# VectorE's block sums of a w_ada load: four instructions in a row, or two halves with a weight remainder between them

## The chip, the cores and the metric

The kernel runs on one core of one Trainium2 chip. The metric is the time of one execution on the device in microseconds (us), of which the median over several executions is compared. The core has a matrix engine (TensorE, PE in the profile), VectorE (DVE), ScalarE (ACT), GpSimd (POOL) and SyncE (SP), each with its own stream of instructions, which meet by semaphores. Transfers from HBM are started by an engine (here by SyncE and by ScalarE) and run on the core's DMA engines.

## The reference

Two transformer blocks in float32 on 256 tokens of width 2048. The first block (eight attention heads of 128 and a gated convolution of 1024 channels) is what matters here. Cut down:

```python
def first_block(x, norm_gain, w_in, conv_w, q_norm_gain, k_norm_gain, ...):
    h = rms_norm(x, norm_gain)
    proj = h @ w_in                       # 256 x 2048 by 2048 x 8192
    h_conv, b_gate, c_gate, z_conv, q, k, v, z_attn = split(proj)
    y_conv = rms_norm(short_gated_conv(h_conv, b_gate, c_gate, conv_w)) * silu(z_conv)
    y_attn = rms_norm(attention(rms_norm(q), rms_norm(k), v)) * silu(z_attn)
    return x + concatenate([y_conv, y_attn]) @ w_out

def ada_modulation(cond, w, b):           # for the second block
    m = silu(cond) @ w + b                # 2048 by 2048 x 12288, for two condition vectors
    return split(m[..., None, :], 6)
```

`silu(c) @ w_ada` doesn't depend on x, so its 96 MB of weights are read and summed beside the first block. The sums of the change are a part of this: a block of w_ada (128 x 2048) times a column of silu(c), added up on VectorE.

## The kernel before

**Weights.** All weights stream in one order. A unit is 128 output columns, in two halves of 512 KB each (K = 8 tiles of 128). A half lands in one of four slots of `raw`. ScalarE copies it rounded into `hi`, VectorE forms the remainder `lo = raw - hi` (the function `split` of either engine, here "a split"; `split(at, j, 0)` is the first half, `split(at, j)` the second; they work two units ahead of TensorE's unit `at, j`). TensorE multiplies with hi and lo. SyncE starts the load of the half three behind in the stream when `lo_done` says that the slot's remainder has been formed, so a remainder that is formed earlier lets a load of 512 KB start earlier.

**Bodies.** The first block runs as 8 head bodies (n = 0 to 7) and 8 convolution bodies (n = 8 to 15) of four units each, written out on each engine in a fixed order. Unit j of a body is evacuated by `both(at, j, dst)`: ScalarE copies one part of the bank G, VectorE adds the other and signals `evac_done`. There are two banks, so TensorE's unit 2 of a body can't begin before `both(at, 0, yq)` of the same body is done.

**Block sums.** Two blocks of w_ada are summed on VectorE in each body: load 2n in the middle, load 2n + 1 at the end. `part_take(m)` waits until load m has landed in the one buffer `ada_raw[:, 1]` and adds its four slices into `part`; with the last of them `ada_taken` rises. ScalarE starts the next load into the same buffer (`part_load`, line 952) when `ada_taken` says that the one before has been taken: load 2n after its second split of unit 0, load 2n + 1 after its split of unit 3, which in a convolution body stands behind a square of the convolution's output (line 1051). So the buffer goes round: taken, issued, landed, taken. After every fourth load TensorE sums `part` over the partitions (`part_sums`).

In a convolution body VectorE forms the convolution's output (`x_new`) behind `part_take(2n)`; ScalarE squares it, and TensorE sums the squares after unit 3 (in the last body between unit 3's halves).

Of the kernel before, what the change touches and what calls it, by code (L numbers as in the profile page):

```python
# [108 lines left out]
def program(nc, t_in, out):  # L109
    with ExitStack() as ctx:  # L110
# [3 lines left out]
        def sem(name):  # L114
            return ctx.enter_context(nc.semaphore(name))
# [94 lines left out]
        ada_full = [sem(f"ada_full{i}") for i in range(2)]  # L210
# [7 lines left out]
        ada_taken, part_summed, part_added = sem("ada_taken"), sem("part_summed"), sem("part_added")  # L218
# [1043 lines left out]
        def _(dve):  # L1262
# [3 lines left out]
            def own(event):  # L1266

                dve.wait_ge(event, turn.next(event.name))
# [4 lines left out]
            def seq(ins):  # L1273

                ins.then_inc(dve_seq, 1)
                dve.wait_ge(dve_seq, turn.next("seq"))

            def tt(dst, a, b, op):
                return dve.tensor_tensor(dst, a, b, op)  # L1279

            def split(at, j, half=1):

                slot = (2 * j + half) % RING
                dve.wait_ge(hi_done, at.unit(j, 5 + half, 2))
                tt(lo[:, slot], raw[:, slot], hi[:, slot], ALU.subtract).then_inc(lo_done, 1)
                own(lo_done)
# [7 lines left out]
            def both(at, j, dst):  # L1294

                dve.wait_ge(half_copied, turn.next("half"))
                tt(dst, dst, G[j % 2][:, 0:T], ALU.add).then_inc(evac_done, 1)
                evacuated(at, j)

            def evacuated(at, j):  # L1300
                dve.wait_ge(evac_done, at.unit(j, 1))
# [67 lines left out]
                ins.then_inc(ada_added, 1)  # L1369
                own(ada_added)  # L1370

            def part_take(n):

                if n % 4 == 0 and n:
                    dve.wait_ge(part_summed, n // 4)
                dve.wait_ge(ada_full[1], 16 * (n + 1))
                k = n % 4 * 4
                for m in range(4):
                    w, c = ada_raw[:, 1, m, :], cpad[:, k + m, 6:7]
                    if k + m == 0:  # L1380
                        seq(dve.tensor_scalar(part[:], w, c, None, ALU.mult))
                    elif m < 3:
                        seq(dve.scalar_tensor_tensor(part[:], w, c, part[:], ALU.mult, ALU.add))
                    else:
                        dve.scalar_tensor_tensor(part[:], w, c, part[:], ALU.mult, ALU.add).then_inc(ada_taken, 1)
                        own(ada_taken)

            def part_add(n):

                dve.wait_ge(part_summed, n + 1)  # L1390
                at = 2 * KT + 4 * n
                tt(adav[:, 0, at:at + 4], PART, col("b_ada", at, 4), ALU.add).then_inc(part_added, 1)
                own(part_added)

            def head_max():
                dve.wait_ge(scores_ready, turn.next("head"))
                dve.reduce_max(sm[:, 0:1], S[0][:, 0:P], AX.X)
                seq(dve.reduce_max(sm[:, 1:2], S[0][:, P:3 * P], AX.X))
                dve.scalar_tensor_tensor(sm[:, 2:4], sm[:, 0:2], -1.0, sm[:, 4:6], ALU.mult, ALU.mult).then_inc(negmax_ready, 1)
                own(negmax_ready)  # L1400

            def head_scale():
                dve.wait_ge(probs_ready, turn.value("head"))
                seq(dve.reciprocal(sm[:, 8:10], sm[:, 6:8]))
                dve.tensor_scalar(P1[:, 0:P], P1[:, 0:P], sm[:, 8:9], None, ALU.mult)
                dve.tensor_scalar(P1[:, P:3 * P], P1[:, P:3 * P], sm[:, 9:10], None, ALU.mult).then_inc(probs_scaled, 1)
                own(probs_scaled)

            def attended(i):

                seq(dve.scalar_tensor_tensor(z_attn[:, i], y_attn[:, i], col("attn_gain", i), z_attn[:, i], ALU.mult, ALU.mult))

            def head_body(n):
                at, prev, h = At(4 * n), n > 0, slice(n, n + 1)
                split(at, 0, 0)
                both(at, 0, yq)
                if prev:
                    head_max()
                split(at, 0)
                if prev:  # L1420
                    head_scale()
                split(at, 1, 0)
                both(at, 1, yk)
                split(at, 1)
                if prev and n % 2 == 0:
                    part_add(n // 2 - 1)
                part_take(2 * n)
                split(at, 2, 0)
                both(at, 2, yv)
                take_sums(sm[:, 36:40], SUMS, add=False)  # L1430
                split(at, 2)
                dve.wait_ge(sum_taken, turn.value("sum"))
                mean_square(sm[:, 36:40], HD1, 4)
                diagonal(2)
                dve.tensor_scalar(sm[:, 4:6], rr[:, 0:2], HD1 ** -0.5, None, ALU.mult)
                split(at, 3, 0)
                evacuated(at, 1)
                dve.tensor_scalar(qg, yq, col("q_gain"), None, ALU.mult)
                dve.wait_ge(bc_ready, turn.value("norm"))
                dve.scalar_tensor_tensor(kn, yk, col("k_gain"), BC, ALU.mult, ALU.mult).then_inc(qk_ready, 1)  # L1440
                own(qk_ready)
                both(at, 3, yz)
                split(at, 3)
                if n == HEADS - 1:
                    ada_add(0, 0)
                silu(z_attn[:, h])
                if prev:
                    take_sums(ss[:, 4:6], SUMS[:, 0:2])
                    attended(n - 1)
                part_take(2 * n + 1)  # L1450

            def normed(tiles, z, n):

# [4 lines left out]
            def conv_body(j):  # L1458
                at, tail, last = At(4 * HEADS + 4 * j), j == 0, j == CONV_TILES - 1
                n = HEADS + j  # L1460
                split(at, 0, 0)
                both(at, 0, yq)
                if tail:
                    head_max()
                split(at, 0)
                if j in (2, 3):
                    b = 4 * (j - 2)
                    low(actB[:, b:b + 4, 0:T], actB[:, b:b + 4, T:2 * T], z_attn[:, b:b + 4], inB, 4)
                if tail:
                    head_scale()  # L1470
                split(at, 1, 0)
                both(at, 1, yk)
                if tail:
                    dve.wait_ge(pad_ready, 1)
                tt(upad[:, 2:2 + T], yk, yq, ALU.mult)
                cw = col("conv_w", 3 * j, 3)
                split(at, 1)
                if n % 2 == 0:
                    part_add(n // 2 - 1)
                if j == 1:  # L1480
                    take_sums(ss[:, 6:8], SUMS[:, 0:2])
                part_take(2 * n)
                split(at, 2, 0)
                both(at, 2, yv)
                seq(dve.tensor_scalar(qg, upad[:, 0:T], cw[:, 0:1], None, ALU.mult))
                seq(dve.scalar_tensor_tensor(qg, upad[:, 1:1 + T], cw[:, 1:2], qg, ALU.mult, ALU.add))
                seq(dve.scalar_tensor_tensor(qg, upad[:, 2:2 + T], cw[:, 2:3], qg, ALU.mult, ALU.add))
                y = y_conv[:, j:j + 1]
                tt(y, qg.rearrange("p (a t) -> p a t", a=1), yv.rearrange("p (a t) -> p a t", a=1), ALU.mult).then_inc(x_new, 1)
                own(x_new)  # L1490
                split(at, 2)
                split(at, 3, 0)
                if last:
                    return
                both(at, 3, yz)
                split(at, 3)
                silu(z_conv[:, j:j + 1])
                dve.wait_ge(z_used, turn.value("z"))
                seq(dve.scalar_tensor_tensor(z_conv[:, j], y_conv[:, j], col("conv_gain", j), z_conv[:, j], ALU.mult, ALU.mult))
                if tail:  # L1500
                    take_sums(ss[:, 4:6], SUMS[:, 0:2])
                    attended(HEADS - 1)
                    mean_square(ss[:, 4:6], HEADS * HD1)
                    diagonal(0)
                else:
                    take_sums(ss[:, 6:8], SUMS[:, 0:2])
                if j in (1, 2):
                    if j == 1:
                        dve.wait_ge(bc_ready, turn.value("norm"))
                    normed(slice(4 * j - 4, 4 * j), z_attn, 4)  # L1510
                part_take(2 * n + 1)


            def lo_first(n):
# [466 lines left out]
```

## Time and profile before

| | |
|---|---|
| median of 3 executions | 1632.04 us (1631.3 to 1637.04) |
| the profiled execution | 1629.51 us, its span 1627.5 us |
| TensorE busy | 1586.5 us, 97% of the span |
| VectorE busy | 1217.0 us, 75% |
| ScalarE busy | 768.8 us, 47% |
| granted TensorE clock, mean | 0.996 |

The profile is of one execution. Busy time is the time in which an engine had an instruction in it; matmuls overlap, so a busy TensorE isn't one at its peak, and what counts is where it waits. The 16 bodies take the stretch from about 35 to 475 us of the span.

### The profile page before, as it was taken

What the parts mean: (1) busy time and instruction counts of PE and PEld (TensorE: products, weight loads), DVE (VectorE), ACT (ScalarE), POOL (GpSimd) and SP (SyncE); (2) the same over time, 40 slices, a digit from 0 to 9 for tenths busy, and PEclk for the clock granted to TensorE, in tenths of its full rate; (3) what the DMA queues carried; (4) which work ended last, traced back from release to release, by engine and by line L of the source; (5) the groups of instructions that cost most, each with busy time, mean ns of one, the idle gap of its engine ahead of it and who ended that gap; (6) DMA issues with size and microseconds to landing.
All of it is one profiled execution on the core that took longest, in us unless ns stands there. A gap on an engine that the chain in (4) does not pass through costs nothing.

```text
span 1627.5 us, 31293 instructions
## 1 busy us (share of the span) xinstructions
PE 1586.5 (97%) x11146; PEld 1430.0 (88%) x11146; DVE 1217.0 (75%) x1816; ACT 768.8 (47%) x1049; POOL 30.5 (2%) x49
## 2 busy tenths in 40 slices
PE   6999999999999999999999999999999999999997
PEld 5788888778889988899899998899989998899986
DVE  7888887898888774788776767776677666556786
ACT  5545444444445554455454554345434553345542
POOL 0000000000001000000000000000000000000000
PEclk9999999999999999999999999999999999999998
DMA  8878877798977778633366657876688666655553
GB/s 314 294 280 288 303 289 278 281 311 321 326 291 215 227 248 300 236 105 104 111 199 192 220 182 215 277 247 185 203 278 253 190 182 190 191 169 181 181 184 112
DMA packets 94545, 372.52 MB, mean 229 GB/s; under 512 B 10016, under 2 KB 10544, under 8 KB 83968
## 3 DMA queue, kind: packets, MB, share of 16 engines
q1 hardware_dynamic: 88656, 333.87, 63.0%
q10 hardware_dynamic: 4608, 33.56, 5.6%
q0 software_dynamic: 1200, 4.02, 0.7%
q8 instruction: 51, 0.84, 0.2%
q14 instruction: 30, 0.25, 0.0%
HBM read 369.30 MB, written 2.10 MB: 228 GB/s over the span
## 4 chain that ended last, share of the span: by engine, by line
issue 72%; PE 24%; DVE 3%; ACT 0%; DMA 0%; POOL 0%; SPq 0%; POOLq 0%; DVEq 0%; ACTq 0%
PE G L438 6%; PE G L440 6%; PE G L439 6%; PE M L756 1%; PE S L743 1%; DVE lo L1279 1%; PE ADA L480 1%; PE S L730 1%; PE ADA L770 0%; PE S L731 0%; DMA ident<-ident_dram 0%; DVE t L1340 0%; DVE resid L1279 0%; PE M L692 0%; DVE actA L1314 0%
## 5 line engine op out<-in xcount | busy, mean ns | idle before, releaser
L902 ACT ACTIVATE hi<-raw 128x1024 fp32r<-128x1024 f32 x496 | 526.3, 1061 | 513.2 <-PE G L440 231.1
L1279 DVE TENSOR_TENSOR lo<-raw,hi 128x1024 fp32r<-128x1024 f32 x496 | 607.3, 1224 | 177.0 <-ACT hi L902 161.6
L438 PE MATMUL G<-actA,hi 128*128 128x258 f32 (+1 forms) x1344 | 382.6, 285 | 1.0 <-DVE actA L1314 0.8
L440 PE MATMUL G<-actA,hi 128*128 128x256 f32 x1344 | 379.2, 282 | 0.0
L439 PE MATMUL G<-actA,lo 128*128 128x258 f32 (+1 forms) x1344 | 378.9, 282 | 0.0
L461 PE MATMUL G<-actA,hi 128*128 128x512 f32 x992 | 357.5, 400 | 3.4 <-DVE W L1279 3.4
L461 PE MATMUL G<-actB,hi 128*128 128x512 f32 x1024 | 355.2, 391 | 0.0
L462 PE MATMUL G<-actB,lo 128*128 128x256 f32 x1024 | 286.7, 280 | 0.0
L462 PE MATMUL G<-actA,lo 128*128 128x256 f32 x992 | 280.6, 283 | 0.0
L438 PEld LDWEIGHTS G<-actA,hi 128*128 128x128 f32 x1344 | 254.3, 189 | 6.2 <-issue 4.2
L439 PEld LDWEIGHTS G<-actA,lo 128*128 128x128 f32 x1344 | 253.8, 189 | 0.2
L440 PEld LDWEIGHTS G<-actA,hi 128*128 128x128 f32 x1344 | 253.6, 189 | 0.0
L461 PEld LDWEIGHTS G<-actA,hi 128*128 128x128 f32 x992 | 187.1, 189 | 56.6 <-issue 11.7
L461 PEld LDWEIGHTS G<-actB,hi 128*128 128x128 f32 x1024 | 191.5, 187 | 41.8
L462 PEld LDWEIGHTS G<-actB,lo 128*128 128x128 f32 x1024 | 193.5, 189 | 0.0
L462 PEld LDWEIGHTS G<-actA,lo 128*128 128x128 f32 x992 | 187.4, 189 | 0.1
L438 PE MATMUL G<-actB,hi 128*128 128x256 f32 x448 | 127.0, 284 | 1.8 <-DVE resid L1787 1.5
L439 PE MATMUL G<-actB,lo 128*128 128x256 f32 x448 | 126.8, 283 | 0.0
L440 PE MATMUL G<-actB,hi 128*128 128x256 f32 x448 | 126.8, 283 | 0.0
L438 PEld LDWEIGHTS G<-actB,hi 128*128 128x128 f32 x448 | 86.0, 192 | 2.2 <-DVE resid L1787 1.7
L439 PEld LDWEIGHTS G<-actB,lo 128*128 128x128 f32 x448 | 86.0, 192 | 0.0
L440 PEld LDWEIGHTS G<-actB,hi 128*128 128x128 f32 x448 | 86.0, 192 | 0.0
(222 smaller groups left out, 1438.1 us busy)
## 6 DMA issues: line engine op xcount, KB each, us to landing
raw<-stream_dram SPq DMA_DIRECT2D x496, 512.0 KB, 4.3
ada_raw<-w_ada_dram SPq DMA_DIRECT2D x64, 1024.0 KB, 6.4
ada_raw<-w_ada_dram ACTq DMA_DIRECT2D x32, 1024.0 KB, 6.3
resid<-xT_dram SPq DMA_DIRECT2D x4, 512.0 KB, 5.5
ctx_tok<-ctx_tok_dram SPq DMA_DIRECT2D x1, 2048.0 KB, 10.1
W<-ctxT_dram POOLq DMA_DIRECT2D x16, 128.0 KB, 4.0
out_dram<-resid SPq DMA_DIRECT2D x4, 512.0 KB, 2.7
ada_raw<-pool_w_dram POOLq DMA_DIRECT2D x1, 1024.0 KB, 7.1
```

The lines of the kernel that those rows point to most:

```text
L438: pe.matmul(wide, hi[:, slot, cols], x[:, k, 0:T + extra], start=(k == 0), stop=False, skip_group_check=True)
L439: pe.matmul(wide, lo[:, slot, cols], x[:, k, 0:T + extra], start=False, stop=False, skip_group_check=True)
L440: m = pe.matmul(bank, hi[:, slot, cols], x[:, k, T + extra:2 * T + extra], start=False, stop=(k == KT - 1), skip_group_check=True)
L461: pe.matmul(bank[:], hi[:, slot, cols], x[:, k, 0:2 * T], start=(k == 0), stop=False, skip_group_check=True)
L462: m = pe.matmul(bank[:, 0:T], lo[:, slot, cols], x[:, k, 0:T], start=False, stop=(k == KT - 1), skip_group_check=True)
L480: m = pe.matmul(ADA[32 * g:32 * g + 32, :], cpad[:, 4 * (k % 4) + g, 6 - 2 * (k // 4):38 - 2 * (k // 4)], ada_raw[:, slot, g, :], start=(k ...
L730: pe.matmul(bank[:, 0:T], q, kT[rows, s, :], start=True, stop=False, skip_group_check=True)
L743: m = pe.transpose(S[c][:, k * P:(k + 1) * P], probs[:, c, k * P:(k + 1) * P], ident[:])
L756: m = pe.matmul(M[64 * h:64 * h + 64, 0:T], v[:, k % 2, g:g + 64], turned[:, h, k, :], start=(k == 0), stop=(k == 3), tile_position=(0, 64 ...
L902: return act.activation(dst, src, ACT.Copy)
L1279: return dve.tensor_tensor(dst, a, b, op)
```

## The change

`part_take(m)` is cut into `part_half(m, False)` (the waits and the slices 0 and 1) and `part_half(m, True)` (the slices 2 and 3, and `ada_taken`). For load 2n the split of unit 2's first half, which stood behind the four slices, now stands between the halves. For load 2n + 1, at the end of a body, the second half goes behind the first split of the next body.

```diff
-            def part_take(n):
-
-                if n % 4 == 0 and n:
-                    dve.wait_ge(part_summed, n // 4)
-                dve.wait_ge(ada_full[1], 16 * (n + 1))
+            def part_half(n, second):
+
+                if not second:
+                    if n % 4 == 0 and n:
+                        dve.wait_ge(part_summed, n // 4)
+                    dve.wait_ge(ada_full[1], 16 * (n + 1))
                 k = n % 4 * 4
-                for m in range(4):
+                for m in ((2, 3) if second else (0, 1)):
...
             def head_body(n):
                 at, prev, h = At(4 * n), n > 0, slice(n, n + 1)
                 split(at, 0, 0)
+                if prev:
+                    part_half(2 * n - 1, True)
                 both(at, 0, yq)
...
-                part_take(2 * n)
+                part_half(2 * n, False)
                 split(at, 2, 0)
+                part_half(2 * n, True)
                 both(at, 2, yv)
...
-                part_take(2 * n + 1)
+                part_half(2 * n + 1, False)
...
             def conv_body(j):
...
                 split(at, 0, 0)
+                part_half(2 * n - 1, True)
                 both(at, 0, yq)
...
-                part_take(2 * n)
+                part_half(2 * n, False)
                 split(at, 2, 0)
+                part_half(2 * n, True)
                 both(at, 2, yv)
...
-                part_take(2 * n + 1)
+                part_half(2 * n + 1, False)
```

The orders of TensorE, ScalarE and SyncE stay as they are. On VectorE, first where body 11 ends and body 12 begins: the sums of load 23, the first split of body 12 (`lo<-raw,hi`) and `both(at, 0, yq)` (`W<-W,G`). Before:

```order
L1383 SCALAR_TENSOR_TENSOR part<-ada_raw,cpad,part 128x512 x3
L1385 SCALAR_TENSOR_TENSOR part<-ada_raw,cpad,part 128x512
L1279 TENSOR_TENSOR lo<-raw,hi 128x1024
L1279 TENSOR_TENSOR W<-W,G 128x256
L1279 TENSOR_TENSOR lo<-raw,hi 128x1024 x2
```

And now, in the same place of VectorE's order:

```order
L1384 SCALAR_TENSOR_TENSOR part<-ada_raw,cpad,part 128x512 x2
L1279 TENSOR_TENSOR lo<-raw,hi 128x1024
L1384 SCALAR_TENSOR_TENSOR part<-ada_raw,cpad,part 128x512
L1386 SCALAR_TENSOR_TENSOR part<-ada_raw,cpad,part 128x512
L1279 TENSOR_TENSOR W<-W,G 128x256
L1279 TENSOR_TENSOR lo<-raw,hi 128x1024 x2
```

The first split has moved ahead of two of the sums; the last sum, which signals `ada_taken`, now stands one split later, and `both(at, 0, yq)` has as much ahead of it as before.

Second, VectorE in the middle of body 12: load 24, between `part_add` (`adav<-S,vec`) and `both(at, 2, yv)`. Before:

```order
L1279 TENSOR_TENSOR adav<-S,vec 128x4
L1381 TENSOR_SCALAR part<-ada_raw,cpad 128x512
L1383 SCALAR_TENSOR_TENSOR part<-ada_raw,cpad,part 128x512 x2
L1385 SCALAR_TENSOR_TENSOR part<-ada_raw,cpad,part 128x512
L1279 TENSOR_TENSOR lo<-raw,hi 128x1024
L1279 TENSOR_TENSOR W<-W,G 128x256
L1485 TENSOR_SCALAR W<-W,vec 128x256
```

And now:

```order
L1279 TENSOR_TENSOR adav<-S,vec 128x4
L1382 TENSOR_SCALAR part<-ada_raw,cpad 128x512
L1384 SCALAR_TENSOR_TENSOR part<-ada_raw,cpad,part 128x512
L1279 TENSOR_TENSOR lo<-raw,hi 128x1024
L1384 SCALAR_TENSOR_TENSOR part<-ada_raw,cpad,part 128x512
L1386 SCALAR_TENSOR_TENSOR part<-ada_raw,cpad,part 128x512
L1279 TENSOR_TENSOR W<-W,G 128x256
L1496 TENSOR_SCALAR W<-W,vec 128x256
```

Here too the split has moved ahead of the last two sums, and what follows `both(at, 2, yv)` has the same instructions ahead of it.

## Rows read from the trace of the kernel before

**Rows 1.** The page's busy times, with their share of the span and the instructions.

```profile
PE 1586.5 (97%) x11146; PEld 1430.0 (88%) x11146; DVE 1217.0 (75%) x1816; ACT 768.8 (47%) x1049; POOL 30.5 (2%) x49
```

**Rows 2.** Waits of TensorE, 0 to 480 us: total, times, longest, in us.

```profile
PE G L461 <- DVE W L1279: 3.4, 2, 2.2
...
PE S L530 <- DVE W L1406: 1.8, 1, 1.8
PE S L509 <- ACT sq L1051: 0.9, 2, 0.5
```

**Rows 3.** The instructions that write `part` and `lo`: durations in ns, or busy us and mean.

```profile
L1383 DVE SCALAR_TENSOR_TENSOR part<-ada_raw,cpad,part x88: 746/752/754, 42.8 to 501.8; 128x512 f32<-128x512 f32 x88
...
L1279 DVE TENSOR_TENSOR lo<-raw,hi 128x1024 fp32r<-128x1024 f32 x496 | 607.3, 1224 | 177.0 <-ACT hi L902 161.6
```

**Rows 4.** Timeline of VectorE, bodies 8 and 9: start, duration, instruction, idle time before it.

```profile
296.02 2.33 DVE L1383 SCALAR_TENSOR_TENSOR part<-ada_raw,cpad,part 128x512 f32<-128x512 f32 x3
...
300.43 0.42 DVE L1279 TENSOR_TENSOR W<-W,G 128x256 f32<-128x256 f32 x1
```

**Rows 5.** Timeline of TensorE, the same columns: the two waits for `both` of unit 0.

```profile
301.00 0.47 PE L461 MATMUL G<-actA,hi 128*128 128x512 f32 x1 [2.24 <-DVE W L1279]
...
355.39 0.47 PE L461 MATMUL G<-actA,hi 128*128 128x512 f32 x1 [1.16 <-DVE W L1279]
```

**Rows 6.** Busy time by engine in one stretch, with granted clock, DMA share and GB/s.

```profile
301.90:305.30 3.40, 3.40 (x12) 2.85 (x11) 3.30 (x5) 0.55 (x1) 0.00 (x0) 0.50 0.97 377
```

**Rows 7.** Timeline of VectorE, bodies 12 to 15.

```profile
379.22 1.23 DVE L1279 TENSOR_TENSOR lo<-raw,hi 128x1024 fp32r<-128x1024 f32 x1
...
386.63 0.49 DVE L1381 TENSOR_SCALAR part<-ada_raw,cpad 128x512 f32<-128x512 f32 x1 [0.95 <-DMA ada_raw<-w_ada_dram]
...
402.23 2.33 DVE L1383 SCALAR_TENSOR_TENSOR part<-ada_raw,cpad,part 128x512 f32<-128x512 f32 x3 [0.97 <-DMA ada_raw<-w_ada_dram]
...
406.64 0.42 DVE L1279 TENSOR_TENSOR W<-W,G 128x256 f32<-128x256 f32 x1
...
411.66 2.33 DVE L1383 SCALAR_TENSOR_TENSOR part<-ada_raw,cpad,part 128x512 f32<-128x512 f32 x3
...
437.28 0.49 DVE L1381 TENSOR_SCALAR part<-ada_raw,cpad 128x512 f32<-128x512 f32 x1
...
447.98 1.23 DVE L1279 TENSOR_TENSOR lo<-raw,hi 128x1024 fp32r<-128x1024 f32 x1 [0.67 <-ACT hi L902]
...
462.02 2.33 DVE L1383 SCALAR_TENSOR_TENSOR part<-ada_raw,cpad,part 128x512 f32<-128x512 f32 x3
```

**Rows 8.** Timeline of ScalarE: its issues of loads 24, 26, 28 and 30, and one copy.

```profile
379.28 0.33 ACTq L952 DMA_DIRECT2D ada_raw<-w_ada_dram  x1
...
387.47 1.06 ACT L902 ACTIVATE hi<-raw 128x1024 fp32r<-128x1024 f32 x1 [4.36 <-DMA raw<-stream_dram]
...
405.43 0.33 ACTq L952 DMA_DIRECT2D ada_raw<-w_ada_dram  x1
...
430.86 0.34 ACTq L952 DMA_DIRECT2D ada_raw<-w_ada_dram  x1
...
455.73 0.33 ACTq L952 DMA_DIRECT2D ada_raw<-w_ada_dram  x1
```

**Rows 9.** DMA issues of 379 to 380, 405 to 406, 430 to 431, 455 to 456 us: KB, us to landing.

```profile
ada_raw<-w_ada_dram ACTq DMA_DIRECT2D x1, 1024.0 KB, 7.2
...
ada_raw<-w_ada_dram ACTq DMA_DIRECT2D x1, 1024.0 KB, 4.9
...
ada_raw<-w_ada_dram ACTq DMA_DIRECT2D x1, 1024.0 KB, 5.6
...
ada_raw<-w_ada_dram ACTq DMA_DIRECT2D x1, 1024.0 KB, 5.7
```

**Rows 10.** Timeline of TensorE: unit 2 of body 13, and body 15's square sums.

```profile
407.55 0.40 PE L461 MATMUL G<-actA,hi 128*128 128x512 f32 x1
...
469.29 0.61 PE L509 MATMUL S<-ones,sq 128*128 128x1 f32 x4 [0.52 <-ACT sq L1051]
```

More of the change, by code:

```diff
@@ L1386, in part_take @@
                         own(ada_taken)
+            def part_take(n):
+                part_half(n, False)
+                part_half(n, True)
             def part_add(n):
```

## The prediction

> **What bounds the kernel now.** I read the busy times first: TensorE is busy in 97% of the span, VectorE in 75% [rows 1]. So the question is where TensorE waits in the 16 bodies, and whether the moved instructions can shorten or lengthen one of those waits. The list of waits answers it: of the waits that VectorE or ScalarE cause in the bodies, the ones near the change are two for `both(at, 0, yq)` before a body's unit 2 (3.4 us together, the longest 2.2), one of 1.8 us for the first head's scaled probabilities (`W` at L1406), and two of 0.9 us together for the squares of a convolution output (L1051) [rows 2]. The timeline places the first two: 301.00 us (2.24 us of idle, body 9) and 355.39 us (1.16 us, body 11) [rows 5]. Behind the longer one the granted clock was 0.50 (1.2 GHz) from 301.9 to 305.3 us [rows 6]: 3.4 us at half speed, in which 1.7 us of work at full speed were done, so 1.7 us were lost. All of it is about 8 us of 1627, which is also about the most that a better order in the bodies could win.
>
> No TensorE wait in the bodies is for a weight remainder (`lo`). That is what the change makes earlier.
>
> **What stays the same: the arithmetic.** The 32 loads still take four instructions each, of 0.75 us (0.49 us for the first of four loads) [rows 3], and nothing is added but the new order. A sum keeps its own start and end whatever its neighbour is, so VectorE's work is unchanged: 0 us.
>
> **What becomes earlier.** Two splits in each body start two sums earlier, 2 x 0.77 = 1.5 us with the step between instructions (2.33 us for three in one row [rows 4]). The remainder itself is worth nothing, since nobody waits for it. The load that it releases is another matter: in body 12 ScalarE sat idle for 4.36 us until the half for `split(at, 2, 0)` landed at about 387.4 [rows 8]. That load was released by the body's first split, which ended at 379.22 + 1.23 = 380.45 [rows 7]. It now starts 1.5 us earlier. This is needed, because the split now comes 1.5 us earlier in VectorE's order too; I cost the pair at nothing. If the cover is gone, that is if the half still landed at 387.4, VectorE would find its copy at 388.5, against 386.63 + 0.49 + 0.77 = 387.9 for the end of the first half: 0.6 us more.
>
> **What doesn't move: `both(at, 0, yq)`.** In body 9 it ends a gapless run that begins with load 17's first sum at 296.02 and ends at 300.43 + 0.42 = 300.85 [rows 4]; TensorE starts 0.15 us later [rows 5]. The same instructions stand ahead of it in the new order. The two largest waits therefore stay: 0 us won.
>
> **What becomes later: the round of the one buffer.** `ada_taken` now comes one split later, 1.22 us for the split [rows 3] and 0.04 for the step between two instructions (2.33 less 3 x 0.75, halved [rows 3, 4]), so 1.26 us. That is so for both loads of a body. For load 2n + 1 it costs nothing at its issue, which is held by the convolution's output, and that has the same work ahead of it. For load 2n it counts: ScalarE waits at `part_load` right for it. Queued behind that wait are ScalarE's copies for unit 1 and, in bodies 10 and 11, the rounding of the attention outputs. VectorE has both (0.45 us with step) and a split (1.26) to do before it needs them, 1.7 us, and ScalarE needs about 1.5 (0.33 for the issue and 1.06 for a copy [rows 8], with steps), so they are just hidden; uncovered they would cost some tenths of a us in a body.
>
> Then the load lands 1.26 us later if its transfer takes as long as before, and at the end of the split chain VectorE arrives as early as before. How much spare time it had, from issue, time to landing and start of the sums [rows 7, 8, 9], in us:
>
> load 24: 379.28 + 7.2 = 386.5, taken from 386.63 with a wait of 0.95, so nothing spare: 1.26 later.
> load 26: 405.43 + 4.9 = 410.3, taken from 411.66: 1.3 spare, nothing more is late.
> load 28: 430.86 + 5.6 = 436.5, taken from 437.28: 0.8 spare, 0.5 more.
> load 30: 455.73 + 5.7 = 461.4, taken from 462.02: 0.6 spare, 0.7 more.
>
> In the earlier convolution bodies I found no sum that waited for its load 2n, and take it as spare enough; in the head bodies VectorE idles behind these sums until TensorE's sums of squares arrive, which swallows a late load. I cost those bodies at nothing; uncovered, one late load there costs up to 1.26 us.
>
> From body 12 on, VectorE has little else to wait for, so a late start is handed on: load 25's sums were already behind a wait of 0.97 us for a load [rows 7] whose issue hangs on the convolution's output, and everything there is 1.26 later. So `both(at, 0, yq)` of body 13 ends at 406.64 + 0.42 + 1.26 = 408.32; TensorE reaches its unit 2 at 407.55 [rows 7, 10] and would start at 408.32 + 0.15 = 408.5: **0.9 us** lost. In body 14 the shift grows to 1.26 + 0.5 = 1.8, of which an idle of 0.67 us that stood before the last split [rows 7] takes away its part: 1.1 is left. In body 15 it grows by 0.7 to 1.8. The convolution's squares were the last to arrive there already, with TensorE 0.52 us idle [rows 10], so TensorE is 1.8 us late at this point: another **0.9 us**. Everything behind it is TensorE's own work and can't give it back. The sum is 0.9 + 0.9 = 1.8 us.
>
> The value 1.26 for load 24 is the upper end for an unchanged transfer. The lower end is 0.9: the two transfers that now swap places ended at 386.5 and 387.4, and if the same bytes flow at the same pace the load of w_ada is now the last of the two. I take 1.26, because a load's time to landing varied more (4.9 to 7.2) [rows 9] than the two ends differ.
>
> How the transfers share is the unknown. In the stretch of rows 6 the DMA engines were 97% busy, and load 24 took 7.2 us where load 26 took 4.9 [rows 9]. The Trainium skill says of this ("DMA: Bandwidth & Descriptors", section "Issuing engines are not separate DMA queues") that transfers started by different engines run on the same 16 DMA engines and interleave; the trace agrees with it, by those two durations. The same page's fit of 2.0 us and the bytes over 436 GB/s would give, as an estimate, 4.4 us for a load alone and nothing that a neighbour adds; with that for load 24 it would have landed in time even now and its term would be 0, so the rows decide against it.
>
> **The sum.** 1629.5 (the profiled execution; 2.0 of it lie outside the span) + 1.8 = 1631.3 us. That execution was 2.5 below the median of the runs shown, so I predict 1632.0 + 1.8 = 1633.8, rounded to 1634.
>
> **Rivals.**
>
> *The earlier weight loads clear the way, a gain (0.17).* If the halves released 1.5 us earlier are out of the way when load 2n + 1 is issued, the waits of 0.95 and 0.97 us and their like in body 11 vanish, and with one the 1.16 us at 355.39 [rows 5]. For it: DMA engines near full. Against it: load 2n + 1 is issued behind the convolution's output, long after the moved releases. Gain 1.2 us there and nothing lost in bodies 13 and 15: 1631.
>
> *Nothing moves (0.27).* The swap costs load 24 less than its transfer's scatter, or TensorE's order hides it: 1632, within 0.5 us.
>
> *Late loads meet the weights, slower (0.10).* Issued behind the released weight half, loads 26, 28 and 30 may each take the 7.2 us of load 24 instead of 4.9, 5.6 and 5.7 [rows 9]: 2.3 + 1.6 + 1.5 = 5.4 us more, and as waits of TensorE grow over 2 us, a piece at half clock, 1.7 us as in rows 6. That is 1.8 + 5.4 + 1.7 = 8.9: 1641. For it: nothing in these bodies refills the spare time. Against it: by the time load 2n is issued, the released half is mostly over, and the next comes 1.6 us after, where it came 1.2 after before. It is slower than before from the point where the added waits pass the 0.5 us that TensorE has in body 13; to be measurably slower it needs all three long transfers.
> [...]
>
> *Likeliest: the sum above (0.46)*, 1632.5 to 1637 by the ends: 0.9 instead of 1.26 takes 0.7 off in two places, and one long transfer of 2.3 us adds that much.
>
> **How the numbers follow.** A measurement tells about 0.5%, 8.2 us, from no change. The first, second and fourth case and most mixtures lie within it; the slower rival is half above and half below by itself, and unknown chains of several late loads I put beside it: slower by over 0.5% has 0.09. Faster by over 0.5% would need all of TensorE's waits in the bodies gone, 0.03. The range goes from 1629, the gain with the lower executions, to 1640, just short of the slower rival.
>
> **What would show it.** Right: `part` sums in pairs with a split between them; the issue of load 24 some 1.3 us further behind the sums of load 23; a wait of about 2.2 us for load 24 in body 12; TensorE idle about 0.9 us before body 13's unit 2 and about 1.4 at body 15's square sums; the waits in bodies 9 and 11 as before, with the half clock behind the former. Wrong: load 24 landing as early as before, or no new wait of TensorE in body 13. The prediction fails upwards if loads 26 to 30 take over 7 us, or if the half clock appears in a second place.

## The result and the profile after

The changed kernel is slower: 1643.94 us median (1641.47 to 1646.06, 4 executions) against 1633.04 us (1631.3 to 1637.04), ratio 1.0063 with a 95% interval of 1.005 to 1.0076. That is 10 us, beyond the range of the forecast (1629 to 1640) and next to the rival that I had given 0.10 (1641).

The page of the changed kernel, answering to [rows 1]; then, further down it, the chain that ended last:

```profile
span 1639.5 us, 31293 instructions
## 1 busy us (share of the span) xinstructions
PE 1590.4 (97%) x11146; PEld 1432.8 (87%) x11146; DVE 1216.9 (74%) x1816; ACT 768.8 (47%) x1049; POOL 30.5 (2%) x49
...
issue 61%; PE 25%; DVE 8%; DMA 5%; ACT 1%; POOL 0%; SPq 0%; POOLq 0%; ACTq 0%; DVEq 0%
```

VectorE's busy time is the same to 0.1 us: no work was added. But transfers now stand in the chain with 5% (0% before), of which `ada_raw<-w_ada_dram` is 4%. The waits of TensorE up to 490 us (total, times, longest), answering to [rows 2]:

```profile
PE M L515 <- DVE W L1320: 4.9, 2, 2.8
PE G L461 <- DVE W L1279: 4.7, 3, 2.2
...
PE S L509 <- ACT sq L1051: 3.8, 2, 2.6
PE S L530 <- DVE W L1412: 1.8, 1, 1.8
```

The squares of the convolution output went from 0.9 to 3.8 us, the additions of `both` have a third wait, and body 0's first broadcast (a matmul of L515, which spreads a row of factors over the partitions) waits 2.8 us. Before, the longest of its line in the bodies was the same broadcast, with 1.6 us (30 to 480 us):

```profile
PE M L515 <- DVE W L1320: 1.9, 2, 1.6
```

VectorE's side of it, from the same view for VectorE, 300 to 475 us:

```profile
DVE part L1384 <- DMA ada_raw<-w_ada_dram: 8.1, 7, 2.3
...
DVE part L1382 <- DMA ada_raw<-w_ada_dram: 2.7, 3, 1.4
```

Ten waits for a load, 10.8 us in this stretch. The kernel before has four there, 4.0 us (three at L1383 and one at L1381). The timeline of VectorE shows where, with the idle time at the end of each row, answering to [rows 7]:

```profile
308.67 1.54 DVE L1384 SCALAR_TENSOR_TENSOR part<-ada_raw,cpad,part 128x512 f32<-128x512 f32 x2 [1.02 <-DMA ada_raw<-w_ada_dram]
...
363.63 1.54 DVE L1384 SCALAR_TENSOR_TENSOR part<-ada_raw,cpad,part 128x512 f32<-128x512 f32 x2 [0.85 <-DMA ada_raw<-w_ada_dram]
...
389.06 0.49 DVE L1382 TENSOR_SCALAR part<-ada_raw,cpad 128x512 f32<-128x512 f32 x1 [0.91 <-DMA ada_raw<-w_ada_dram]
...
415.15 1.54 DVE L1384 SCALAR_TENSOR_TENSOR part<-ada_raw,cpad,part 128x512 f32<-128x512 f32 x2 [1.23 <-DMA ada_raw<-w_ada_dram]
...
442.16 0.49 DVE L1382 TENSOR_SCALAR part<-ada_raw,cpad 128x512 f32<-128x512 f32 x1 [1.36 <-DMA ada_raw<-w_ada_dram]
...
459.04 1.54 DVE L1384 SCALAR_TENSOR_TENSOR part<-ada_raw,cpad,part 128x512 f32<-128x512 f32 x2 [2.26 <-DMA ada_raw<-w_ada_dram]
463.45 0.42 DVE L1279 TENSOR_TENSOR W<-W,G 128x256 f32<-128x256 f32 x1
...
469.20 1.54 DVE L1384 SCALAR_TENSOR_TENSOR part<-ada_raw,cpad,part 128x512 f32<-128x512 f32 x2 [0.77 <-DMA ada_raw<-w_ada_dram]
```

Loads 18, 20 (0.4 us, not shown), 22, 26, 28 and 30, which VectorE found ready before, now keep it waiting. The wait for load 24 is what it was: 0.91 us, for 0.95. It was issued late and took 5.9 us where it had taken 7.2, so it landed at 388.93, which is 386.5 again once the 2.5 us are taken off by which the whole program was late. The row of its transfer in the changed kernel:

```profile
ada_raw<-w_ada_dram ACTq DMA_DIRECT2D x1, 1024.0 KB, 5.9
```

And the issue of load 26 on ScalarE with its time to landing, answering to [rows 8] and [rows 9]:

```profile
408.99 0.34 ACTq L952 DMA_DIRECT2D ada_raw<-w_ada_dram  x1
```

```profile
ada_raw<-w_ada_dram ACTq DMA_DIRECT2D x1, 1024.0 KB, 6.1
```

It took 6.1 us where it took 4.9 before. Two rows of TensorE's timeline show what arrives last in body 15, answering to [rows 10], and the windows view the granted clock behind the second:

```profile
464.01 0.47 PE L461 MATMUL G<-actA,hi 128*128 128x512 f32 x1 [1.74 <-DVE W L1279]
...
476.47 0.27 PE L509 MATMUL S<-ones,sq 128*128 128x1 f32 x1 [2.62 <-ACT sq L1051]
```

```profile
477.90:481.30 3.40, 3.40 (x12) 2.85 (x12) 1.85 (x5) 0.60 (x1) 1.92 (x3) 0.50 0.94 328
1440.50:1447.30 6.80, 6.80 (x33) 6.80 (x33) 0.00 (x0) 0.00 (x0) 0.00 (x0) 0.50 0.33 98
```

**The account.** TensorE has the same 11146 matmuls in the same order in both kernels, so the start of one in one trace less its start in the other says how much has been lost by then: 0.8 us in the program's first loads, ahead of anything changed; 2.0 from body 0's broadcast on; 2.5 at the end of body 11; 2.8 in body 14; 5.0 at body 15's unit 2; 7.2 at its square sums; 8.2 behind the half clock at 478; 8.3 up to 1432 and 11.4 behind the half clock at 1440. So the bodies cost 1.2 + 5.2 = 6.4 us and the clock behind them 1.0. The last 3.1 us are no part of the change: of the 16 profiles of this study 14 have a piece at half clock near 1435, of 3.4 or 6.8 us, the kernel before run once more (control) among them. The profile of before that the prediction was read from is one of the two without it. The 7.4 us are of two single executions, and that of the changed kernel is its fastest of four; the medians lie 10 us apart, and the other 3 us or so have no trace.

### The profile page after: what moved, and what is told of

Same layout as the page of the kernel before. It is cut to its first block, busy times and chain, and to the rows that moved or that the text cites. A ratio compares the mean times of both kernels' runs of the same rounds, so it can differ in the third digit from the quotient of the medians.

```text
span 1639.5 us, 31293 instructions
## 1 busy us (share of the span) xinstructions
PE 1590.4 (97%) x11146; PEld 1432.8 (87%) x11146; DVE 1216.9 (74%) x1816; ACT 768.8 (47%) x1049; POOL 30.5 (2%) x49
## 4 chain that ended last, share of the span: by engine, by line
issue 61%; PE 25%; DVE 8%; DMA 5%; ACT 1%; POOL 0%; SPq 0%; POOLq 0%; ACTq 0%; DVEq 0%
PE G L438 6%; PE G L440 6%; PE G L439 6%; DMA ada_raw<-w_ada_dram 4%; DVE lo L1279 2%; DVE part L1384 2%; PE M L756 1%; PE S L743 1%; PE ADA L480 1%; ACT hi L902 1%; DVE part L1386 1%; PE S L730 1%; DVE mix L1279 1%; DMA ident<-ident_dram 0%; DVE W L1357 0%
```

## The experiments

All ratios are to executions of the kernel before on the same chips. A ratio of 1.001 is 1.6 us.

**control** is the kernel before, unchanged.

> The kernel before once more, under a label of its own, to see how far two sets of executions of one program lie apart and whether TensorE's clock falls to half near 1435 us (the sums of gate_part), where it did in the profile of the changed kernel and not in that of before. If the fall belongs to the change: ratio 1.000, mean granted clock 0.996, no fall there. If it is chance: ratio 1.000 all the same, but some executions with a mean clock of 0.993 to 0.994 and 3 to 4 us longer.

1634.12 us (1630.07 to 1637.67, 12 executions), ratio 0.9996 (0.9981 to 1.0012). Mean clocks from 0.991 to 0.997, so the fall near 1435 us comes and goes in one program. It is chance here:

```profile
1437.50:1440.90 3.40, 3.40 (x19) 3.40 (x18) 0.00 (x0) 0.21 (x1) 0.00 (x0) 0.50 0.24 90
```

Its profile also had one wait of 2.6 us at the square sums of body 15, so the kernel before stands close to that edge itself.

**mid_only** and **boundary_only** each do one half of the change. In mid_only:

```diff
                 split(at, 0, 0)
-                part_half(2 * n - 1, True)
                 both(at, 0, yq)
...
-                part_half(2 * n + 1, False)
+                part_take(2 * n + 1)
```

> Only the sums of loads 2n (middle of a body) are split; those at a body's end stay whole and stand ahead of the next body's first split. Theory L (the later ada_taken at the boundary makes loads 2n late, and that is most of the loss): ada_taken for load 2n + 1 comes where it did, so loads 2n are on time; only body 0 loses its 1.2 us in front of the first broadcast: plus 1 to 2.5 us on 1633. Rival S (VectorE waits for ScalarE's copy of the split that was pulled forward): the split of unit 2 is the one pulled forward against a late copy, so this half carries the most, plus 5 to 8 us.

In boundary_only:

```diff
-                part_half(2 * n, False)
-                split(at, 2, 0)
-                part_half(2 * n, True)
+                part_take(2 * n)
+                split(at, 2, 0)
```

> Only the sums of loads 2n + 1 (end of a body) are split around the next body's first split; those in the middle stay whole. Theory L: the issue of every load 2n comes 1.26 us later and the loss of the convolution bodies is all here, plus 5 to 8 us, with TensorE idle before unit 2 of body 15 and at its square sums, and none of the extra 1.2 us before the first broadcast. Rival S: plus 0 to 2 us.

mid_only: 1634.5 us, ratio 1.0009 (0.9993 to 1.0024). boundary_only: 1643.33 us, ratio 1.0063 (1.0041 to 1.0085), the whole loss, and more than the 5 to 8 us expected. The waits for loads (L1384 and L1382) tell the same, 300 to 475 us, first in mid_only:

```profile
DVE part L1384 <- DMA ada_raw<-w_ada_dram: 1.2, 2, 0.9
```

and in boundary_only, with TensorE's wait for the squares below:

```profile
DVE part L1384 <- DMA ada_raw<-w_ada_dram: 8.1, 6, 3.2
...
DVE part L1382 <- DMA ada_raw<-w_ada_dram: 3.1, 2, 1.8
```

```profile
PE S L509 <- ACT sq L1051: 7.1, 3, 4.9
```

So the cost is at the boundary: at the load that it makes late, not at the split in the middle.

**heads_only** and **conv_only** do the change in one kind of body. heads_only, in the convolution bodies (conv_only does the like in the head bodies):

```diff
                 split(at, 0, 0)
-                part_half(2 * n - 1, True)
+                if j == 0:
+                    part_half(2 * n - 1, True)
                 both(at, 0, yq)
...
-                part_half(2 * n, False)
-                split(at, 2, 0)
-                part_half(2 * n, True)
+                part_take(2 * n)
+                split(at, 2, 0)
...
-                part_half(2 * n + 1, False)
+                part_take(2 * n + 1)
```

> The change in the head bodies alone (with the boundary into body 8); the convolution bodies keep whole sums. Theory L: head bodies have an idle stretch on VectorE behind the sums, so late loads cost nothing there and only body 0's 1.2 us are lost: plus 1 to 2 us. Rival: each head body loses some tenths at its scaled probabilities, plus 3 to 5 us.

> The change in the convolution bodies alone (boundaries from body 8 into 9 on). Theory L: plus 5 to 8 us, all by the end of body 15; the first broadcast as before. Rival: plus 3 us or less.

heads_only: 1634.89 us, ratio 1.0009 (0.9995 to 1.0023). conv_only: 1642.41 us, ratio 1.0048 (1.0032 to 1.0065). As expected: late loads cost nothing in head bodies. VectorE waits for loads in the head bodies of heads_only only three times, 0.9 us in all (up to 300 us; its other six waits, 4.7 us, lie in the convolution bodies, which are as before). In its profile TensorE is 2.5 us late at body 0's broadcast and, when the wait for the first head's probabilities has swallowed a piece at half clock, stays so from 68 us to body 8.

**body0_whole** sums load 0 in one piece ahead of the split.

```diff
                 part_half(2 * n, False)
+                if not prev:
+                    part_half(2 * n, True)
                 split(at, 2, 0)
-                part_half(2 * n, True)
+                if prev:
+                    part_half(2 * n, True)
```

> The changed kernel, with load 0 of body 0 summed in one piece ahead of the split of unit 2. Both theories: TensorE's wait for the first broadcast (near 52 us) shrinks from 2.8 to 1.6 us and the time falls by 1.2 us against the changed kernel: 1642 to 1643 where that stood at 1644. If the 1.2 us were the start's scatter and no part of the change, nothing falls.

1642.5 us, ratio 1.0058 (1.0036 to 1.0079). The 1.2 us are too few for the medians, but the trace has them: TensorE's wait for body 0's broadcast is 1.4 us (1.6 in the kernel before), not 2.8. The cause is in VectorE's timeline of the changed kernel, body 0:

```profile
43.48 0.75 DVE L1384 SCALAR_TENSOR_TENSOR part<-ada_raw,cpad,part 128x512 f32<-128x512 f32 x1
45.58 1.23 DVE L1279 TENSOR_TENSOR lo<-raw,hi 128x1024 fp32r<-128x1024 f32 x1 [1.35 <-ACT hi L902]
46.84 0.75 DVE L1384 SCALAR_TENSOR_TENSOR part<-ada_raw,cpad,part 128x512 f32<-128x512 f32 x1
```

The split was pulled ahead of its copy: ScalarE is then at the squares of a context tile,

```profile
42.38 1.92 ACT L1108 ACTIVATE ctx_tok<-ctx_tok 128x2048 f32<-128x2048 f32 x1
...
44.41 1.06 ACT L902 ACTIVATE hi<-raw 128x1024 fp32r<-128x1024 f32 x1
```

and VectorE, with two sums queued behind the split, stood idle for 1.35 us.

**small_after** and **small_before** fetch a quarter of each load, so that every load is early. The modulation values aren't the reference's in either.

```diff
-                act.dma_start(ada_raw[:, 1].rearrange("p k n -> p (k n)"), src).then_inc(ada_full[1], 16)
+                act.dma_start(ada_raw[:, 1, 0], src[:, 0:512]).then_inc(ada_full[1], 16)
```

> The changed kernel, but ScalarE's loads from the second on fetch only the first of four slices (256 KB instead of 1 MB); the sums run over what stands in the buffer, so the modulation values are not the reference's. The instructions are the same. Theory L: loads land before VectorE comes in every body, so splitting costs only body 0's 1.2 us: within 2 us of the same cut on the kernel before, near 1633 or below. Rival S (waits for copies, not for loads): the distance of 8 to 11 us to the kernel with the same cut stays.

> The kernel before with the same smaller loads (one slice of four fetched, sums over what stands there, so the modulation values are not the reference's), the reference point for the changed kernel with smaller loads. Both theories: 1 to 2 us faster than the kernel before, because the waits of about 1 us for loads 21, 25 and 27 go and with them TensorE's 1.2 us in body 11.

small_after: 1633.91 us, ratio 0.9994 (0.998 to 1.0007). small_before: 1631.34 us, ratio 0.9982 (0.997 to 0.9994). The distance between the two is 2.6 us where it was 10 (at most 2 were expected; body 0 has 1.2 of it). With the new order on VectorE in place, but no load to wait for, the loss of the convolution bodies is gone. small_before also shows what there was to win: with every load early and a quarter as large, the kernel before gains 2 to 3 us. TensorE's waits for the squares in small_after:

```profile
PE S L509 <- ACT sq L1051: 0.9, 2, 0.5
```

**late_issue** is the other way round: VectorE's order of before, but ScalarE's issue held back.

```diff
                 act.wait_ge(ada_taken, n)
+                if n % 2 == 0:
+                    act.wait_ge(lo_done, 4 * n + 5)
```

> The kernel before, with VectorE's order untouched; ScalarE's issue of each load 2n waits for the first split of the body as well as for ada_taken, so it comes 1.25 us later, as in the changed kernel. Theory L: nothing of the loss needs the new order on VectorE, so plus 5 to 10 us, with the same waits of TensorE at the end of the convolution bodies. Rival O (it is the order on VectorE, with its steps and neighbours, that costs): plus 0 to 2 us.

1639.4 us (1635.12 to 1644.8), ratio 1.0037 (1.0023 to 1.0051): 6 us, with no instruction of VectorE moved. The rival of the order is dead. By the medians the loss is less than the boundary's, though the issue is equally late; the two intervals overlap. The profiled execution is one of its slower ones (1643.15 us), and VectorE waits for loads in it longer than in boundary_only, 13.2 us for 11.2 (L1385 and L1383), 300 to 475 us:

```profile
DVE part L1385 <- DMA ada_raw<-w_ada_dram: 10.4, 7, 2.0
...
DVE part L1383 <- DMA ada_raw<-w_ada_dram: 2.8, 2, 1.5
```

**release_after** splits at the boundary only, and holds back the weight half that the split releases, so that it is queued behind load 2n as before.

```diff
+                if 4 <= u < UNITS_IN and u % 4 == 0:
+                    sp.wait_ge(evac_done, u + 1)
                 weight(2 * u % RING, 2 * u + 8)
```

> Only the boundary sums split, and SyncE starts the half that the pulled-forward split releases only when both for unit 0 is done, that is behind ScalarE's issue of load 2n, in the order that the kernel before has. The issue stays 1.26 us late. If the transfers of loads 2n became longer because the weight half is now queued in front of them (boundary only: 5.7 to 8.0 us where they took 4.8 to 5.7), they are 5 to 6 us again and what is left is the lateness alone: plus 1.5 to 4 us on 1633. If the later issue alone makes them longer (other neighbours in the queue), the time stays near the 1643 of the boundary alone.

1635.27 us (1633.76 to 1639.18), ratio 1.002 (1.0009 to 1.0031): of the boundary's 10 us 2 to 3 are left. The transfer of load 26, time to landing last, first in boundary_only:

```profile
ada_raw<-w_ada_dram ACTq DMA_DIRECT2D x1, 1024.0 KB, 7.1
```

in late_issue:

```profile
ada_raw<-w_ada_dram ACTq DMA_DIRECT2D x1, 1024.0 KB, 6.3
```

and in release_after:

```profile
ada_raw<-w_ada_dram ACTq DMA_DIRECT2D x1, 1024.0 KB, 4.9
```

Over the seven even loads 18 to 30 the mean is 5.4 us before, 6.2 in the changed kernel, 6.7 in boundary_only, 6.5 in late_issue and 4.9 in release_after (4.8 to 4.9 each). In late_issue the weight half and the load are started by the same event; in release_after the load goes first. So within these kernels what lengthens the transfer is less the later hour than the half in front of it or beside it.

One profile seems to speak against it: control's mean is 6.3, with 7.2 to 7.8 us for its last three even loads and 5.0 to 5.9 for the others. There is a third stream to look at. SyncE's queue also carries loads of 1 MB of w_ada, which TensorE sums itself, and one of them is mostly in flight when ScalarE issues its load. That of load 24 in the kernel before, issued at 375.80, 3.5 us ahead of it, took

```profile
ada_raw<-w_ada_dram SPq DMA_DIRECT2D x1, 1024.0 KB, 6.6
```

and so was under way for the first 3.2 us of load 24, which took 7.2. For control's last three even loads it was 3.2 to 4.2 us. In the five profiles with no weight half just in front (before, control, mid_only, heads_only, swap_before) 9 of the 35 even loads 18 to 30 took over 6.5 us, and all 9 had that neighbour beside them for 2.9 us or more; of the other 26 only 4 had. This is read from the traces; no run varied it.

Load 18 separates the two neighbours, since in all of these profiles SyncE's load of 1 MB is over when it is issued (within 0.1 us):

| load 18 | us to landing |
|---|---|
| no weight half ahead of it: before, control, mid_only, heads_only, swap_before, release_after | 4.9, 5.0, 5.0, 4.6, 5.1, 4.8 |
| weight half 1.6 us ahead: changed kernel, boundary_only, conv_only, body0_whole | 6.1, 5.7, 6.7, 5.5 |
| both by one event: late_issue | 6.2 |

The first row has early issues and a late one (release_after), the others only late ones. So the half is worth some 0.4 to 2 us.

release_after doesn't price the lateness by itself, though. Its transfers are shorter than those of the kernel before, and in its profile VectorE waits for no load 2n at all, only for loads 23 and 25, which took 8.2 and 8.8 us:

```profile
DVE part L1386 <- DMA ada_raw<-w_ada_dram: 4.1, 2, 2.3
```

What TensorE loses there between bodies 11 and 13, 1.8 us, stands behind these two waits. So by this profile an issue 1.26 us late costs nothing at the loads 2n if they then take 4.9 us; why loads 23 and 25 were slow is open.

**half_loads** issues each load as two of 512 KB, each when its half of the buffer is free.

```diff
+                act.wait_ge(ada_taken, 2 * n - 1)
+                act.dma_start(ada_raw[:, 1, 0:2].rearrange("p k n -> p (k n)"), src[:, 0:1024]).then_inc(ada_full[1], 16)
+                act.wait_ge(ada_taken, 2 * n)
+                act.dma_start(ada_raw[:, 1, 2:4].rearrange("p k n -> p (k n)"), src[:, 1024:2048]).then_inc(ada_full_b, 16)
```

> The changed kernel with each load of w_ada issued as two transfers of 512 KB, each as soon as the half that it overwrites has been summed, and each half of the sums waiting for its own transfer. Theory L: the first half is now issued 1.5 us earlier than in the kernel before and the second 1.26 us later, so VectorE hardly waits: the loss of the convolution bodies goes, 1630 to 1635. Rival: two transfers cost more on the queues than they save, 1638 or more.

1635.37 us, ratio 1.0011 (1.0 to 1.0021), with two waits for loads, 1.7 us, in the convolution bodies. That is just above what was expected (1630 to 1635). The change can be had at nearly no loss, but there is no gain behind it.

**swap_before** (in the kernel before) puts `both(at, 0, yq)` ahead of the split in the convolution bodies.

```diff
-                split(at, 0, 0)
                 both(at, 0, yq)
+                split(at, 0, 0)
```

> The kernel before, with both for unit 0 ahead of the body's first split in the convolution bodies (the split that nobody waits for steps behind the addition that TensorE waits for). TensorE's waits before unit 2 of bodies 9 and 11 shrink by a split, 1.25 us: 2.2 to 1.0 and 1.2 to 0. With the half clock behind the first gone too: 1629 to 1631. Rival: the split comes 0.45 us later, with it a weight load, and the gain is taken back at the square sums: 1632 to 1634.

1635.18 us, ratio 1.0011 (0.9996 to 1.0025): no gain, and the expectation's "split that nobody waits for" was wrong. TensorE waits as long in front of unit 2, now for the remainder:

```profile
302.76 0.51 PE L461 MATMUL G<-actA,hi 128*128 128x512 f32 x1 [2.13 <-DVE lo L1279]
```

The body's first split forms unit 2's own first half; it had been done 0.45 us ahead of the addition, which hid that wait. In body 11 the wait did go, from 1.16 to 0.17 us, and the total shows nothing of it.

**half_both** has half_loads, load 0 whole, and the order split, both, second half; **take_behind** has the whole boundary sums behind both.

```diff
                 split(at, 0, 0)
-                part_half(2 * n - 1, True)
                 both(at, 0, yq)
+                part_half(2 * n - 1, True)
```

> Loads issued in halves, load 0 of body 0 summed whole, and in the convolution bodies the order split, both for unit 0, second half of the sums. TensorE waits before unit 2 of body 9 for both; this now comes two sums, 1.55 us, earlier: the wait goes from 2.2 to about 0.7 us, the one in body 11 goes, body 0's 1.2 us don't arise, and the half clock behind body 9 may go with the longer wait (1.7 us). Theory: 1629 to 1632, 0.1 to 0.3% below the kernel before. Rival: the part_sums and the load's second half, 0.45 us later still, give it back: 1633 to 1635.

> As half_both, but from body 9 on the whole of the boundary's sums stands behind both for unit 0. The addition is another 1.55 us earlier, so TensorE no longer waits before unit 2 at all; the second half of load 2n - 1 is used 0.45 us later than in half_both, but the first half 3.2 us later, so the first transfer of load 2n loses its head start. If the addition decides: 1628 to 1631. If the load decides: VectorE waits for loads 2n again and the time is above half_both's by 1 to 4 us.

(half_both's; in take_behind the first half of the boundary's sums goes there too, from body 9 on.)

half_both: 1635.45 us, ratio 1.0013 (1.0002 to 1.0025); take_behind: 1634.45 us, ratio 1.0005 (0.9992 to 1.0018). half_both came out next to its rival; of take_behind's two cases neither came, since it is neither faster nor slower than half_both and VectorE waits for a load only once, 0.4 us. The wait in front of body 9's unit 2 did shrink in half_both, from 2.24 to 1.17 us, without half clock behind it,

```profile
301.15 0.47 PE L462 MATMUL G<-actA,hi 128*128 128x512 f32 x1 [1.17 <-DVE W L1283]
```

but TensorE then waited 5.8 us in all for the squares (L510) and 1.1 for the sums of `part` (L499):

```profile
PE S L510 <- ACT sq L1054: 5.8, 3, 2.5
...
PE S L499 <- DVE part L1392: 1.1, 1, 1.1
```

take_behind has 3.1 us for the squares, 1.1 for `part` and, before body 9's unit 2, 1.1 us for the remainder `lo`, so the addition isn't the last to arrive there any more.

As I read these rows, VectorE itself is the one that is late in the convolution bodies (argued from the waits, not tried apart): whatever goes forward in its order pushes something else back that TensorE needs half a body later. No version that computes the same values beat the kernel before.

## Why the prediction was wrong

**Right.** No work added; nobody waits for the remainders as they stood; `both(at, 0, yq)` of body 9 is where it was and its wait the same; the issue of load 24 came 1.26 us late (383.01 against 379.28, less the 2.5 us by which TensorE's whole program was late by then); the buffer's round is the mechanism, and load 2n the one that suffers (boundary_only against mid_only); head bodies swallow it (heads_only).

**The step that failed** is the price of the late load, "the load lands 1.26 us later if its transfer takes as long as before", with its counter-argument in the slower rival, "by the time load 2n is issued, the released half is mostly over". It was in front: released 1.6 us ahead of the load, it was in flight until 1.8 to 3.1 us behind the load's issue (loads 18 to 30 of the changed kernel). Load 26 took 6.1 us in the changed kernel and 7.1 at the boundary alone, for 4.9. Of the 10 us that boundary_only costs, 7 to 8 go when the half is put behind the load again and the issue stays late (release_after). I had written of the half released 1.5 us earlier only as help for its own split.

**Load 24, right in its issue and wrong in its landing.** The sum began with load 24 landing 1.26 us later, a wait of 2.2 us for it and 0.9 us of TensorE before body 13's unit 2. It landed as early as before, its wait stayed (0.91 for 0.95), and there is no wait of TensorE in body 13: both signs that I had named for being wrong. I carried its 7.2 us over as if they belonged to the load; in the changed kernel it took 5.9, with SyncE's load of 1 MB beside it for 1.9 us instead of 3.2. That the total is above my sum and not below it is due to the other loads.

**The spare in the earlier bodies.** "In the earlier convolution bodies I found no sum that waited for its load 2n, and take it as spare enough": loads 18, 20 and 22 had 1.5, 2.7 and 2.8 us to spare (landing to first sum in the trace of before), which was enough for 1.26 us and not for the longer transfers as well (load 18: 4.9 to 6.1, load 22: 4.8 to 7.0). They were then waited for 1.02, 0.38 and 0.85 us. That cost TensorE only some 0.5 us up to body 11; the loss comes in bodies 14 and 15.

**The split pulled forward, costed at nothing.** True in the convolution bodies, wrong in body 0, by 1.2 us: I looked for the copy in body 12 and not where ScalarE's order is another one, and I left body 0's broadcast (1.6 us of wait) out of the list of waits near the change.

**Terms.** Forecast 0.9 us in front of a unit 2 and 0.9 at body 15's square sums; measured 2.2 by unit 2 of body 15 (not 13; 1.74 of it are the idle time of the row at 464.01) and 2.2 at the squares. The half clock behind the longer wait was in the rival, with 1.7 us; it cost 1.0. That rival came nearest, in its number (1641) and its cause, but not in its terms: loads 26, 28 and 30 were to take 7.2 us each and took 6.1, 6.4 and 5.6, and load 29 (8.7 us, a wait of 2.26) was in nobody's sum.

**The Trainium skill's rule** that DMAs of different engines share the same 16 DMA engines ("DMA: Bandwidth & Descriptors", "Issuing engines are not separate DMA queues") was cited and not carried into the sum. Here 0.5 MB issued ahead of 1 MB on another engine's queue, or together with it, made it 1.4 to 2.2 us longer (load 26, late_issue and boundary_only against release_after). The same page of the Trainium skill gives its fit (4.4 us for 1 MB) for transfers issued by GpSimd; these are ScalarE's, and the shortest in these traces took 4.6.

**What stays open.** Why the remaining 2 to 3 us of release_after fall behind loads 23 and 25. How much SyncE's loads of 1 MB cost a neighbour, since no run moved them. And whether boundary_only and late_issue differ at all: their medians are 4 us apart and their intervals overlap; that the half is 1.5 us further ahead in the one is the difference between them, but no run varied that distance alone.

## What to carry to other kernels

When a reordering lets a transfer start earlier, ask what it will stand in front of: a buffer that goes round (taken, issued, landed, taken) with a microsecond or two to spare, as here, can take a late issue or a longer transfer, but not both. Before splitting a group of instructions whose last one frees a buffer, add up the whole round, take the transfer's time with its new neighbours and not the old ones, and check each body's spare, also where the trace shows no wait. Don't carry one load's long transfer over as its own: list what else was in flight beside it, on every queue. And something that nobody waits for is worth nothing earlier: moving it up pushes back what somebody does wait for.

## What the runs showed of the hardware

One program's executions scatter with TensorE's granted clock: control had mean clocks from 0.991 to 0.997 and times from 1630.07 to 1637.67 us. Near 1435 us, where TensorE sums `gate_part` in 16 matmuls of one column each (32 in the trace), the granted clock was 0.50 (1.2 GHz) for 0, 3.4 or 6.8 us in profiles of nearly the same program; 6.8 us cost 3.1 in the changed kernel. A wait of 2.2 us in front of body 9's unit 2 was followed by half clock in the profile of before and not in control's; of the 14 profiles with a wait of 2.1 to 2.7 us there, 10 have a piece at half clock at that place and 4 have none. A difference of 3 us between two single profiles says nothing here.

A transfer's time depended on what else was in flight, on whichever engine's queue: load 18 (1 MB, ScalarE) took 4.6 to 5.1 us with no weight half just ahead, 5.5 to 6.7 with one.
